# Four attention output tiles side by side in one PSUM bank, evacuated and normed as one

## What is computed

```python
h = rms_norm(x, pre_mix_norm)
proj = h @ w_in
fox_o = forgetting_attention(fq, fk, fv, log_f)           # 8 heads x 64, causal, query blocks of 128
fox_o = rms_norm(fox_o, fox_out_norm).reshape(b, s, D_FOX)
gdn_o = gated_delta_chunked(cq, ck, cv, g, beta)          # 4 heads x 128
gdn_o = (rms_norm(gdn_o, gdn_out_norm) * gate).reshape(b, s, D_GDN)
mixed = jnp.concatenate([fox_o, gdn_o], axis=-1) @ w_out
x = x + rms_norm(mixed, post_mix_norm)
h = rms_norm(x, pre_mlp_norm)
y = jnp.square(jax.nn.relu(h @ w_up)) @ w_down
x = x + rms_norm(y, post_mlp_norm)
```

## Time and profile before

| | |
|---|---|
| median of 3 runs | 1470.46 us (1466.90 to 1472.14) |
| span of the profiled execution | 1465.4 us |
| TensorE busy over the span | 1379.2 us (94%) |
| VectorE busy | 944.7 us (64%) |
| ScalarE busy | 658.4 us (45%) |
| GpSimd busy | 573.6 us (39%) |
| the chain that ended last | 76% TensorE, 10% VectorE, 4% GpSimd, 2% ScalarE |

### The profile page before, as it was taken

The page is one execution under the profiler, slowest core; times in us unless marked ns, Lnnn a source line. Parts: engine busy times, 40 slices in busy tenths (PEclk is TensorE's granted clock), DMA queues, the critical chain, the costliest instruction groups (busy, mean ns, idle before and its releaser), DMA issues.

```text
span 1465.4 us, 20680 instructions
## 1 busy us (share of the span) xinstructions
PE 1379.2 (94%) x7379; PEld 1165.7 (80%) x7379; DVE 944.7 (64%) x1506; ACT 658.4 (45%) x1404; POOL 573.6 (39%) x470
## 2 busy tenths in 40 slices
PE   5999999998989899898899889999999999999997
PEld 4778888877989899797688768888888778888885
DVE  6977777765567665765545799655655584444557
ACT  6654334435455555555433532333233344445453
POOL 3733322314152441614401377665564164442001
PEclk9999999998999999999999999999999999999999
DMA  7143333245113131013222244444442995333533
GB/s 207 47 129 103 115 115 115 88 151 179 30 59 102 49 97 44 16 44 102 87 73 86 85 125 159 158 158 159 158 158 102 329 320 168 94 99 105 202 98 144
DMA packets 135325, 177.88 MB, mean 121 GB/s; under 512 B 10492, under 2 KB 82732, under 8 KB 135224
## 3 DMA queue, kind: packets, MB, share of 16 engines
q1 hardware_dynamic: 135224, 176.56, 37.5%
HBM read 124.05 MB, written 52.48 MB: 120 GB/s over the span
## 4 chain that ended last, share of the span: by engine, by line
PE 76%; DVE 10%; issue 5%; POOL 4%; ACT 2%; DMA 2%; SPq 1%; DVEq 0%; POOLq 0%; ACTq 0%
PE ps L2717 7%; PE ps L3018 7%; PE ps L3020 7%; PE ps L3019 7%; PE ps L3031 6%; PE ps L3032 6%; PE ps L3033 6%; PE ps L2668 5%; PE ps L2670 5%; PE ps L2669 5%; PE ps L2860 3%; PE ps L2970 2%; PE ps L2972 2%; PE ps L2971 2%; PE ps L2722 2%
## 5 line engine op out<-in xcount | busy, mean ns | idle before, releaser
L3031 PE MATMUL ps<-db_hi,da_hi 128*128 128x512 f32 x448 | 175.3, 391 | 4.1 <-DVE db_lo L2288 4.0
L3032 PE MATMUL ps<-db_lo,da_hi 128*128 128x512 f32 x448 | 174.4, 389 | 0.0
L3033 PE MATMUL ps<-db_hi,da_lo 128*128 128x512 f32 x448 | 174.3, 389 | 0.0
L2286 DVE TENSOR_TENSOR da_lo<-a_raw,da_hi 128x512 fp32r<-128x512 f32 x112 | 85.6, 764 | 121.3 <-ACT da_hi L1756 121.2
L1756 ACT ACTIVATE da_hi<-a_raw 128x512 fp32r<-128x512 f32 x112 | 70.7, 631 | 159.3 <-PE ps L3033 136.9
L3018 PE MATMUL ps<-bt_hi,ring_hi 128*128 128x512 f32 x320 | 127.2, 397 | 5.3 <-DVE ring_lo L2208 5.2
L3020 PE MATMUL ps<-bt_hi,ring_lo 128*128 128x512 f32 x320 | 126.0, 394 | 0.0
L3019 PE MATMUL ps<-bt_lo,ring_hi 128*128 128x512 f32 x320 | 125.4, 392 | 0.0
L2668 PE MATMUL ps<-i_bt_hi,i_ring_hi 128*128 128x512 f32 x280 | 111.0, 396 | 3.2 <-DVE i_ring_lo L1848 1.8
L2670 PE MATMUL ps<-i_bt_hi,i_ring_lo 128*128 128x512 f32 x280 | 110.3, 394 | 0.0
L2669 PE MATMUL ps<-i_bt_lo,i_ring_hi 128*128 128x512 f32 x280 | 110.0, 393 | 0.0
(11 more groups left out here) (367 smaller groups left out, 3655.2 us busy)
## 6 DMA issues: line engine op xcount, KB each, us to landing
a_raw<-act_dram SPq DMA_DIRECT2D x112, 256.0 KB, 2.6
act_dram<-s_act SPq DMA_DIRECT2D x64, 256.0 KB, 2.2
wd<-in_w_down_dram SPq DMA_DIRECT2D x15, 1024.0 KB, 7.7
act_dram<-c SPq DMA_DIRECT2D x48, 256.0 KB, 4.8
...
```

The lines of the kernel that those rows point to most:

```text
L3031: nc.tensor.matmul(acc, da_hi[s][:, cols], db_hi[s][:, :], start=start, stop=False, skip_group_check=True)
L3032: nc.tensor.matmul(acc, da_hi[s][:, cols], db_lo[s][:, :], start=False, stop=False, skip_group_check=True)
L3033: return nc.tensor.matmul(acc, da_lo[s][:, cols], db_hi[s][:, :], start=False, stop=stop, skip_group_check=True)
```

## The change

The four tiles of a group now lie side by side in bank 7: tile i has 64 columns at place i mod 8, so that a head fills the bank's 512 columns, and a group (half a head) 256 of them. Bank 2 is not used for outputs any more. ScalarE does nothing for a tile until the group's fourth product is done. Then it copies all 256 columns at once, waits for that copy, and squares the 256 columns in place in PSUM, without a sum. VectorE sums the squares by a reduction in front of `fox_rr`, and norms the four tiles by two instructions of 256 columns: times `fox_ms`, then, after a wait for the first, times the norm's weights. They have one place in the plan, 6.0 behind v (3.6 for the last group), where there were four.

TensorE's wait changes too. It no longer waits for `fox_read` at each tile. At the first tile of each group but the very first it waits for `tail_mean` of the group before, which is the writing of `fox_ms`, since both groups lie in one bank.

The core of the diff:

```diff
@@ -224,7 +224,8 @@
             at("pe", v, "pv", i, 1)
         else:
             v = u
-        at("act", v + 0.7, "out", i)
+        if qb % HT == HT - 1:
+            at("act", v + 0.7, "out", i)
         if qb == 4 and n + 1 < 2 * GDN_HEADS:
             at("act", b + 0.5, "k_hi", n + 1)
             at("dve", b + 1.8, "k_lo", n + 1)
@@ -234,8 +235,7 @@
             tail = ("fox", n, qb // HT)
             at("dve", v + 1.9, "tail_mean", tail)
             at("pool", v + 2.0, "tail_power", tail)
-            for k in range(HT):
-                at("dve", v + (3.6 + 0.3 * k if i == NFT - 1 else 5.0 + 1.5 * k), "tail_norm", "fox", (n, qb - HT + 1 + k))
+            at("dve", v + (3.6 if i == NFT - 1 else 6.0), "tail_norm", "fox", (n, qb // HT))
 
 
 for _p in range(GDN_HEADS):
@@ -262,6 +262,7 @@
 FOX_RR = numbered([tail for tail in MEAN if tail[0] == "fox"])
 NORMS = [item[1:] for item in ORDER["dve"] if item[0] == "tail_norm"]
 NORM = numbered(NORMS)
+FOX_NORM = numbered([norm for norm in NORMS if norm[0] == "fox"])
 
 
 
@@ -270,7 +271,6 @@
 _free = max(n for n, item in enumerate(_items) if item[0] == "fill")
 LATE_SCANS = [item[1:] for item in _items[_free:] if item[0] == "scan_o"]
 LATE_TURNS = [FOX_CHUNK[item[1:]] for item in _items[_free:] if item[0] == "turn"]
-LATE_TILES = [item[1] for item in _items[_free:] if item[0] == "pv" and item[2] == 0]
 LATE_OUT = numbered(LATE_SCANS)
 
 
@@ -279,18 +279,12 @@
     return 3 if n in LATE_TURNS and n % 2 == 1 else 6
 
 
-def out_bank(i):
-
-    return 2 if i in LATE_TILES and i % 2 == 1 else 7
-
-
 TURN_BEFORE = {n: max((m for m in range(n) if turn_bank(m) == turn_bank(n)), default=None) for n in range(NFC)}
-OUT_BEFORE = {i: max((j for j in range(i) if out_bank(j) == out_bank(i)), default=None) for i in range(NFT)}
 
 
 def norms_of(t):
 
-    return max(count for (_, (_, tile)), count in NORM.items() if tile == t)
+    return max(count for (what, (_, part)), count in NORM.items() if part == (t if what == "gdn" else t // HT))
 
 
 
@@ -471,7 +465,6 @@
         q_lo = [placed(f"q_lo{s}", 140416 + 512 * s, [P, P], F32R) for s in range(2)]
         state = placed("state", 141440, [P, P])
         v_new = placed("v_new", 141952, [P, P])
-        sq_fox = placed("sq_fox", 142464, [P, FOX_DIM])
         sq_gdn = placed("sq_gdn", 142720, [P, P])
         SMALL = 143232
         g_last = [placed(f"g_last{s}", SMALL + 32 * s, [P, NCHUNK]) for s in range(2)]
@@ -515,7 +508,12 @@
             return banks(turn_bank(n))
 
         def fox_o(i):
-            return banks(out_bank(i))
+
+            return banks(7)[:, i % NT * FOX_DIM:(i % NT + 1) * FOX_DIM]
+
+        def fox_o4(n, half):
+
+            return banks(7)[:, half * HT * FOX_DIM:(half + 1) * HT * FOX_DIM].rearrange("p (t d) -> p t d", t=HT)
 
         def bank(f):
             return fills[f % NFILL_BANKS]
@@ -627,7 +625,9 @@
         pt_act = sem("pt_act")
         pt_dve = sem("pt_dve")
         fox_pv = sem("fox_pv")
+        fox_copied = sem("fox_copied")
         fox_read = sem("fox_read")
+        fox_scaled = sem("fox_scaled")
         gdn_square_done = sem("gdn_square_done")
         rr_ready = sem("rr_ready")
         norm_sum = sem("norm_sum")
@@ -1504,16 +1504,16 @@
             def fox_out(i):
 
                 h, hh, qb = FOX_TILES[i]
+                half = qb // HT
                 act.wait_ge(fox_pv, last_chunk(i) + 1)
-                if i == 0:
+                if i == HT - 1:
                     for s in range(2):
                         act.wait_ge(proj_stored[s], stores_of(NPAIR - 2 + s))
-                if i == HT:
+                if i == NT - 1:
                     act.wait_ge(filled, FILL[(0, "v", 1, 0)])
-                nc.scalar.activation(mixed_fox(qb // HT, h)[:, qb % HT, hh * FOX_DIM:(hh + 1) * FOX_DIM], fox_o(i)[:, 0:FOX_DIM], ACT.Copy)
-                if i >= 1:
-                    act.wait_ge(fox_read, i)
-                nc.scalar.activation(sq_fox[:, :], fox_o(i)[:, 0:FOX_DIM], ACT.Square, accum_out=fox_ss[:, hh, qb:qb + 1]).then_inc(fox_read, 1)
+                nc.scalar.activation(mixed_fox(half, h)[:, :, hh * FOX_DIM:(hh + 1) * FOX_DIM], fox_o4(i // NT, half), ACT.Copy).then_inc(fox_copied, 1)
+                act.wait_ge(fox_copied, i // HT + 1)
+                nc.scalar.activation(fox_o4(i // NT, half), fox_o4(i // NT, half), ACT.Square).then_inc(fox_read, 1)
 
             def o_out(h, c):
 
@@ -2077,19 +2077,21 @@
                     nc.vector.tensor_scalar(gdn_ms[:, cols], gdn_ss[:, cols], GDN_DIM * EPS, None, ALU.add).then_inc(tail_mean, 1)
                     return
                 r, rr = row_sum[:, n % 2, cols], fox_rr[:, n % 2, cols]
-                dve.wait_ge(fox_read, n * NT + (half + 1) * HT)
+                dve.wait_ge(fox_read, 2 * n + half + 1)
+                nc.vector.tensor_reduce(fox_ss[:, n % 2, cols], fox_o4(n, half), AX_X, ALU.add).then_inc(rr_ready, 1)
                 nc.vector.scalar_tensor_tensor(out=rr, in0=r, scalar=FOX_DIM * EPS, in1=r, op0=ALU.mult, op1=ALU.mult).then_inc(rr_ready, 1)
-                dve.wait_ge(rr_ready, FOX_RR[tail])
+                dve.wait_ge(rr_ready, 2 * FOX_RR[tail])
                 nc.vector.tensor_tensor(fox_ms[:, n % 2, cols], fox_ss[:, n % 2, cols], rr, ALU.add).then_inc(tail_mean, 1)
 
-            def fox_norm(n, qb):
+            def fox_norm(n, half):
 
                 h, hh = divmod(n, 2)
-                dve.wait_ge(tail_power, TAIL[("fox", n, qb // HT)])
+                dve.wait_ge(tail_power, TAIL[("fox", n, half)])
                 dve.wait_ge(masks_ready, 4)
-                o = mixed_fox(qb // HT, h)[:, qb % HT, hh * FOX_DIM:(hh + 1) * FOX_DIM]
-                nc.vector.scalar_tensor_tensor(out=o, in0=o, scalar=fox_ms[:, n % 2, qb:qb + 1], in1=fox_norm_row[:, :],
-                                               op0=ALU.mult, op1=ALU.mult).then_inc(mixed_ready, 1)
+                o = mixed_fox(half, h)[:, :, hh * FOX_DIM:(hh + 1) * FOX_DIM]
+                nc.vector.tensor_tensor(o, o, wide(fox_ms[:, n % 2, half * HT:(half + 1) * HT], FOX_DIM), ALU.mult).then_inc(fox_scaled, 1)
+                dve.wait_ge(fox_scaled, FOX_NORM[("fox", (n, half))])
+                nc.vector.tensor_tensor(o, o, stacked(fox_norm_row[:, :], HT), ALU.mult).then_inc(mixed_ready, 1)
 
             def gdn_norm(h, c):
 
@@ -2850,14 +2852,12 @@
                 n, (h, hh, qb) = FOX_CHUNK[(i, c)], FOX_TILES[i]
                 wait_copied(n)
                 if c == 0:
-                    if OUT_BEFORE[i] is not None:
-                        pe.wait_ge(fox_read, OUT_BEFORE[i] + 1)
-                    if i == LATE_TILES[0]:
-                        fills_read()
+                    if i >= HT and qb % HT == 0:
+                        pe.wait_ge(tail_mean, MEAN[("fox", (i - HT) // NT, 1 - qb // HT)])
                     if hh == 0 and qb == 0:
                         pe.wait_ge(act_prep, ACT_PREP[("read", (h, "fv", 1, 0))])
                 for kb in range(4 * c, min(4 * c + 4, qb + 1)):
-                    last = nc.tensor.matmul(fox_o(i)[:, 0:FOX_DIM], probs_t[n % 2][:, kb - 4 * c, :], v_tok[h % 2][:, kb, hh * FOX_DIM:(hh + 1) * FOX_DIM],
+                    last = nc.tensor.matmul(fox_o(i), probs_t[n % 2][:, kb - 4 * c, :], v_tok[h % 2][:, kb, hh * FOX_DIM:(hh + 1) * FOX_DIM],
                                             start=(kb == 0), stop=(kb == qb))
                 last.then_inc(fox_pv, 1)
 
@@ -2941,7 +2941,7 @@
                     pe.wait_ge(state_ready, GDN_HEADS * NCHUNK)
                     pe.wait_ge(o_read, GDN_HEADS * NCHUNK)
                 elif t == 1:
-                    pe.wait_ge(fox_read, NFT)
+                    pe.wait_ge(tail_mean, MEAN[("fox", 2 * GDN_HEADS - 1, 1)])
                 if t >= 2:
                     pe.wait_ge(m_lo_ready, t)
                 for k in range(KT):
```

## The result

The changed kernel takes 1484.83 us (median of 4 runs, 1482.93 to 1485.02) against 1471.01 of the kernel before, run beside it: a ratio of 1.0095, with a 95% interval of 1.0080 to 1.0109. It is 13.8 us slower. I had written 1474.9, with a range up to 1481.0: the sign was right, the size was not, and the time lies outside the range.

What follows compares the result with a forecast made beforehand. TensorE was taken to set the pace in the attention stage. Terms 5.4 - 1.1 + 0.6 - 1.0 - 0.5 + 1.0 = +4.4 us on 1470.46 gave 1474.9 us, range 1466 to 1481.

Steps and rivals of the forecast that it cites:

- The new wait: TensorE's first product of a group waits for fox_ms: stops at eight places, 8.8 us gross, 5.4 us net.
- What is given back: While TensorE stands, other engines catch up and some later waits shrink: a fifth of the net stops, -1.1 us.
- the stops are absorbed: Rival: TensorE's later waits shrink by nearly the whole stop; -0.9 us, 1469.6 us; chance 18%.
- the clock falls with the stops: Rival: full stops in TensorE plus one or two clock falls of 1.7 us; +10 to +13, 1481 us; chance 13%.
- The norms on VectorE: Two wide norms replace four narrow ones; with the added reductions VectorE gains at most 3.6 us; taken as -1.0 us.
- ScalarE's freed queue: 48 of 64 output pairs no longer stand before the next probs_t or q_hi on ScalarE; taken as -0.5 us.
- fewer, larger instructions win: Rival: ScalarE's and VectorE's savings come back and the stops give nothing net; -5.0 us, 1465.5 us; chance 9%.
- The stage's end: Last group's chain before the output projection: ScalarE 0.2, reduction 0.42, norms 0; +0.6 us.
- The clock: TensorE's new stops can bring or move a half-clock fall, 1.7 us each; between -1.7 and +3.4, taken as +1.0 us.
- The base: Starting time for the sum: the median of three runs, 1470.46 us, 5.1 us above the profile's span of 1465.4.

Runs made afterwards that it cites:

- wait_only: Kernel before, plus one line: TensorE's first product of each group also waits for fox_ms of the group before; 1477.33 us, ratio 1.0039.
- wide_norm: Kernel before with only the norm changed: two instructions of 256 columns at plan place 6.0 instead of four of 64; 1479.93 us, ratio 1.0068.
- narrow_norm: Changed kernel with the old norm: four instructions of 64 columns at their old places; 1478.52 us, ratio 1.0049.
- wide_spread: Kernel before with the wide pair of norms taken apart, at plan places 5.0 and 9.5 (last group together); 1472.43 us, ratio 1.0011.
- clumped_norm: Kernel before with a group's four narrow norms all at plan place 6.0 (3.6 for the last group); 1481.42 us, ratio 1.0067.
- before_again: Kernel before, unchanged, profiled a second time; 1467.13 us, span 1465.3.

## Why the prediction was wrong

**The new wait** was found in the right places with about the right size. I summed stops of 8.8 us gross and 5.4 net; the changed kernel stands 6.9 us for `fox_ms` in front of L2860 (5.8 by name, 1.1 under "issue") and 0.5 in front of L2948. Two of my places make up most of it: 1.96 us at 592 (exactly the gross number; the 2.09 of waiting for `qn` there is gone in return) and 2.56 at 690, for which I had 3.06 gross. Four of the small stops showed too, at 0.47, 0.81, 0.53 and 0.54 us for 0.62, 0.97, 0.74 and 0.73. The one of 0.03 didn't, nor the one at 702, where TensorE waits 1.20 us for ScalarE's `probs_t` instead.

**What is given back** was 1.1 us in my sum. wait_only shows 3.4 of 5.2 us of waiting given back, yet costs 6.2 us. The rival "the stops are absorbed" described TensorE's idle time well (+1.8), and the rival "the clock falls with the stops" named what came on top: 0.0025 of clock, 2.3 us by the line. I had held the two to exclude each other, and they don't. Together they make 4.1 of the 6.2 us; the rest stays open.

**The norms on VectorE** are the step that failed: "Between 0 and -3 us; I take -1.0". Measured, the wide pair costs +8.8 us by itself (wide_norm) and 6.5 of the changed kernel's 13.8 (narrow_norm). Two errors are in it. The price of a pair, 0.87, was held only against four narrow norms at the stage's end, where GpSimd had nothing to run beside them; I had seen `fox_rr` take 1.50 us, called the old norms "stretched here and there", and charged the new ones with no stretch at all (16 x 0.87). And I costed the busy time alone, while the change also moves four places in VectorE's queue into one. What is queued behind that place I never looked up, though the order of VectorE's instructions above shows, behind the pair, `t_inv` and the `probs_t` copy; at head 2 it is `xb` and that copy. wide_spread and clumped_norm separate the errors: the wide form costs 1.3 us, and the rest is the place. Of the 8.8 us, TensorE's idle time shows 5.6 (4.0 of them for `probs_t`), the clock's line gives 1.9, and 1.3 us I can't assign.

**ScalarE's freed queue**, -0.5, didn't come: TensorE's waits for its `probs_t` are 2.5 us, against 1.7. The wide copy and square are not what made them longer: wait_only and wide_norm, with the narrow ones, have 2.6.

**The rival "fewer, larger instructions win"** took its fixed part from ScalarE's rows. The norms have one too: alone, 0.28 us for 64 columns in the kernel before and 0.42 for 256 in wide_norm. So four narrow ones cost more than a wide pair where nothing holds them, and VectorE was busy 19.2 us with norms in the changed kernel for 24.2 before. That saving is real; TensorE didn't wait for it, and the place of the pair cost more.

**The stage's end**, +0.6, was right. In the changed kernel (timeline):

```profile
733.24 1.50 PE L2860 MATMUL ps<-v_tok,probs_t 128*128 128x64 f32 x12
...
735.20 0.37 ACT L1516 ACTIVATE ps<-ps 128x256 f32<-128x256 f32 x1
...
735.72 0.41 DVE L2081 TENSOR_REDUCE fox_ss<-ps 128x4 f32<-128x256 f32 x1
...
737.98 0.42 DVE L2094 TENSOR_TENSOR mixed_half<-mixed_half,fox_norm_row 128x256 f32<-128x256 f32 x1
...
740.85 0.70 PE L2970 MATMUL ps<-big_hi,m_hi 128*128 128x512 f32 x1 [3.23 <-DVE m_lo L2164]
```

From the end of the last product with V (734.74) to that of the last norm (738.40) it is 3.7 us; before it was 3.0 (718.55 to the end of the row at 720.68). Here, with GpSimd idle beside it, a wide norm does take 0.42.

**The clock**, +1.0, was too small and its rival too weak. The medians fell from 0.983 to 0.980, by the line above 2.8 us; by the two profiled executions (half of 13.6) it would be up to 6.8. One fall costs about 1.1 us by the line, not the 1.7 that I charged; there were more of them.

**The base.** I wrote that the median "lies 5.1 us above" the profile's span, 1465.4, and added the sum to the median. A span in fact lies 1.8 us under its own run's time; the profiled execution was one of the shortest, as before_again's was, at clocks of 0.986 and 0.987 where the median has 0.983. That did no harm to the forecast, but it hid how far executions of the same program differ, 1467 to 1478 us here, partly with the clock.

With the terms put right the sum is: wait 6.2 (wait_only), norms in one place 8.8 (wide_norm), and 1.1 for the one bank, the wide copy and square and the reduction together (narrow_norm less wait_only), 16.1 against 13.8 measured. The parts overlap by some 2 us, which stays open, as does the part of the clock in each: one profile of each kernel doesn't fix it. No kernel here beats the kernel before; the nearest with wide norms is wide_spread, at +0.1%.
